# The first three weight units of a map, instead of two, run together over the arriving input tiles (second block of a two-block network on one NeuronCore)

## The chip, the cores and the metric

The kernel is one program on one core of a Trainium2 chip. The metric is device time in microseconds (us) of one execution; lower is better. TensorE (PE in the rows) does the matrix products, VectorE (DVE) and ScalarE (ACT) the elementwise work, GpSimd (POOL) almost nothing here, and SyncE (SP) issues nearly all DMAs.

## The reference, cut to what matters

The program computes two blocks one after the other over 512 positions of width 1024, all in float32. The second block, the one that is changed, is this, for two layers (`ab` in the first, `c` in the second):

```python
for layer in range(DEPTH):
    hn = rmsnorm(h, gains[0])
    mix = mixer_ab(hn, ...) if layer % 2 == 0 else mixer_c(hn, ...)   # each: hn @ w_in, attention-like work, @ w_out
    h = h + rmsnorm(mix, gains[1])
    hn = rmsnorm(h, gains[2])
    ff = jnp.square(jax.nn.relu(hn @ w_up[layer])) @ w_down[layer]    # 1024 -> 4096 -> 1024
    h = h + rmsnorm(ff, gains[3])
    gate = jax.nn.sigmoid(h @ w_ple_gate[layer])
    h = h + gate * (p[layer] @ w_ple[layer])
```

What matters is that each layer holds several large products `activations @ weights` (here called maps), most of them right behind a normalisation.

## The kernel before, in words

**A map.** Activations lie transposed: a tile is 128 features by 512 positions, and 1024 features are 8 tiles. Weights come as units of 128 x 1024 floats, each of which gives 128 output features from 8 input tiles. The function `linear` runs one map: `count` units over the tiles. Float32 precision is had from three products of rounded pieces: weights are split into a high part `WHI` (ScalarE, L378) and a rest `WLO` (VectorE, L387), activations in the same way, and each pair of unit and tile takes three matmuls of 128x512 (L431). So a unit is 8 x 3 = 24 matmuls.

**Weight buffers.** Units arrive by DMA in a ring of `SLOTS` = 2 buffers (`fetch`, L366), and are split into one of `WSLOTS` = 3 slots. `split_hi` waits until the unit that had the slot three units ago has been finished by TensorE (`units_done`); `fetch` waits until a ring buffer has been split (`w_lo`). Both engines run the same `turns`: before the first output, `split(c, eng, pos + WSLOTS)` makes the first three units ready as far as that has not been done; then for every finished unit `j` the output is taken off PSUM (`take`), unit `j + 3` is split, and the rest of the work on output `j` follows (`then`). A map ends by having split the first two units of the next map; the third is the one that the next map's own `turns` begins with.

**Order.** There is no scheduler. Each engine executes its instructions in the order in which the Python code emits them, block after block: `normalize` (or `pieces`) emits its ScalarE and VectorE work for all 8 tiles, and `linear`, called after it, emits `turns` behind that. On TensorE, `begin(j)` waits until the PSUM bank of unit `j` is free and its weights are split; `ready(k)` waits for the input tile `k`. The parameter `group` says how many units run together over the tiles as they arrive: tile 0 for each of them, then tile 1, and so on. The other units follow one by one:

```python
        for j in range(group):
            begin(j)
        for k in range(kt):
            pe.wait_ge(*ready(k))
            for j in range(group):
                products(j, k)
        for j in range(group, count):
            begin(j)
            for k in range(kt):
                products(j, k)
```

**What makes the tiles.** `normalize` (root of the mean square, then L694 scales a tile on VectorE, L683 rounds it on ScalarE, L707 takes the rest on VectorE) stands before `project_a`, `project_c` and the first up-projection of `ffn2`. `pieces` (L743 rounds on ScalarE, L750 takes the rest on VectorE) stands before `project_b` and `mix_out`. In `project_a` the outputs go through a convolution of four taps: L1647 on ScalarE, then three instructions of L1664 on VectorE, all of it in `take`, ahead of the next split. In `ffn2` the hidden width 4096 is worked off in four parts `p` of 8 units up and 8 down; only for the first part do the tiles still arrive, the other three find them ready.

Of the kernel before, what the change touches and what calls it, by code (L numbers as in the profile page):

```python
# [16 lines left out]
KT = D // P  # L17
NL, NC = 512, 256
# [119 lines left out]
def ffn_parts(hidden_tiles):  # L138

    return [(p, min(UB, hidden_tiles - p)) for p in range(0, hidden_tiles, UB)]  # L140
# [1493 lines left out]
def project_a(c, args, xp, ready):  # L1634

    CV = A2["CV"]
    tap3, taps, silu, zed = c.mark("act", 12), c.mark("dve", 36), c.mark("act", 12), c.mark("act", 4)
    cv = lambda j, lo, n: c.a(CV + (j % 4) * NL + lo, n)
    out = lambda j: c.a(A2["Q"] + j * NL, NL)
    tap = lambda k, j: c.vec(f"conv{k}", j)  # L1640

    def scalar(act, j, acc):
        a = acc[0][0]
        if j >= 12:
            act.activation(out(j), a, ACT.Silu).then_inc(*zed.up())
        else:
            act.activation(cv(j, 0, NL), a, ACT.Identity, scale=tap(3, j)).then_inc(*tap3.up())  # L1647

    def scalar2(act, j):
        if 1 <= j <= 12:  # L1650
            act.wait_ge(*taps.at(3 * j))
            act.activation(out(j - 1), cv(j - 1, 0, NL), ACT.Silu).then_inc(*silu.up())

    def vector(dve, j, acc):
        if j >= 12:
            return
        a = acc[0][0]
        dve.wait_ge(*tap3.at(j + 1))
        for z, k in enumerate((2, 1, 0)):
            d = 3 - k  # L1660
            if z:
                dve.wait_ge(*taps.at(3 * j + z))
            y = cv(j, d, NL - d)
            dve.scalar_tensor_tensor(y, a[:, 0:NL - d], tap(k, j), y, ALU.mult, ALU.add).then_inc(*taps.up())  # L1664

    linear(c, args, xp, KT, 16, NL, ready, lambda j: zed.at(j - 11) if j >= 12 else taps.at(3 * j + 3), scalar, vector, scalar2)


def project_b(c, args, xp, ready):

    done = c.mark("act", 16)

    def scalar(act, j, acc):
        i, m = j // 4, j % 4
        dst = c.a(A2[("Q", "K", "Z", "V")[i]] + m * NL, NL)
        if i == 2:
            act.activation(dst, acc[0][0], ACT.Sigmoid).then_inc(*done.up())
        else:
            act.activation(dst, acc[0][0], ACT.Copy, scale=SCALE2 if i == 0 else 1.0).then_inc(*done.up())
    linear(c, args, xp, KT, 16, NL, ready, lambda j: done.at(j + 1), scalar)  # L1680


def project_c(c, args, xp, ready):

    done = c.mark("act", 12)

    def scalar(act, j, acc):
        act.activation(c.a(place_c(j), NL), acc[0][0], ACT.Identity, bias=c.vec("b_qkv", j)).then_inc(*done.up())
    linear(c, args, xp, KT, 12, NL, ready, lambda j: done.at(j + 1), scalar)


def unit_norms(c, tiles_of, scales, eps=EPS, gain=None, times=None):
# [471 lines left out]
def place_c(j):  # L2164

    o = A3
    return o["Q"] + j * NL if j < 8 else o["K"] + (j - 8) * (NL + P) + P if j < 10 else o["VT"] + (j - 10) * NL
# [258 lines left out]
def mix_out(c, args, xp, ready, dst, bias=None):  # L2426

    squares = Squares(c, KT, NL, D)
    done = c.mark("act", KT)

    def scalar(act, j, acc):
        a = acc[0][0]
        if bias is None:
            act.activation(dst(j), a, ACT.Copy).then_inc(*done.up())
        else:
            act.activation(dst(j), a, ACT.Identity, bias=c.vec(bias, j)).then_inc(*done.up())

    def scalar2(act, j):
        squares.square(act, j, dst(j), done.at(j + 1))

    def vector2(dve, j):
        if j >= 2:
            squares.add(dve, j - 1)
    linear(c, args, xp, KT, KT, NL, ready, lambda j: done.at(j + 1), scalar, None, scalar2, vector2)
    return squares


# [41 lines left out]
def ffn2(c, args, l, late, last):  # L2489


    with c.pair(NL) as xp, c.pair(NL) as hidden, c.room(4 * NL) as room, c.room(2 * D) as wp, c.room(2 * NL) as pl, \
            c.room(KT * NL) as emb:
        hh, hl, hw = hidden
        y = lambda k: c.h(k)
        re = lambda j: room[:, (j % 4) * NL:(j % 4 + 1) * NL]
        ready = normalize(c, late, lambda k, q: c.vec(f"gain{l}2", k), xp)
        loaded = c.mark("dma", 2)
        block = c.stage()

        @block.sync
        def _(sp):
            sp.wait_ge(c.units_done, c.pos)
            sp.dma_start(wp[:], args["wple"][l]).then_inc(*loaded.up())
            sp.dma_start(pl[:], args["ple"][l]).then_inc(*loaded.up())
        full = lambda k: (c.units_done, c.pos)
        for p, m in ffn_parts(32):
            relu, made, hi, lo = c.mark("act", m), c.mark("dve", m), c.mark("act", m), c.mark("dve", m)
            done = c.mark("dve", KT)
            squares = Squares(c, KT, NL, D) if p + m == 32 else None  # L2510
            emptied = c.pos

            def scalar(act, j, acc):
                if j >= 4:
                    act.wait_ge(*lo.at(j - 3))
                act.activation(re(j), acc[0][0], ACT.Relu).then_inc(*relu.up())  # L2516

            def vector(dve, j, acc):
                dve.wait_ge(*relu.at(j + 1))
                dve.tensor_tensor(re(j), acc[0][0], re(j), ALU.mult).then_inc(*made.up())  # L2520

            def scalar2(act, j):
                act.wait_ge(*made.at(j + 1))
                if j == 0:
                    act.wait_ge(c.units_done, emptied)
                act.activation(hh[:, j * hw:j * hw + NL], re(j), ACT.Copy).then_inc(*hi.up())

            def vector2(dve, j):
                dve.wait_ge(*hi.at(j + 1))
                q = slice(j * hw, j * hw + NL)  # L2530
                dve.tensor_tensor(hl[:, q], re(j), hh[:, q].bitcast(F32), ALU.subtract).then_inc(*lo.up())
            linear(c, args, xp, KT, m, NL, ready, lambda j: made.at(j + 1), scalar, vector, scalar2, vector2)
            ready = full

            def take(dve, j, acc):
                a = acc[0][0]
                if p == 0:
                    dve.tensor_copy(y(j), a).then_inc(*done.up())
                else:
                    dve.tensor_tensor(y(j), y(j), a, ALU.add).then_inc(*done.up())  # L2540

            def square(act, j):
                if squares is not None:
                    squares.square(act, j, y(j), done.at(j + 1))

            def add(dve, j):
                if squares is not None and j >= 2:
                    squares.add(dve, j - 1)
            linear(c, args, hidden, m, KT, NL, lambda k: lo.at(k + 1), lambda j: done.at(j + 1), None, take, square, add)
        ready = add_normed(c, squares, f"gain{l}3", y, xp=xp)  # L2550
        return gated_embedding(c, args, l, xp, ready, loaded, wp, pl, emb, room, last)
# [60 lines left out]
def block2(c, args, late):  # L2612
# [28 lines left out]
    late = LateSquares(c, KT, NL, D)  # L2641
    add_normed(c, squares, "gain01", c.h, late=late)
    squares = ffn2(c, args, 0, late, False)
    o = A3
    with c.low_room(o["HIGH"]):
        with c.pair(NL) as xp:
            ready = normalize(c, squares, lambda k, q: c.vec("gain10", k), xp)
            project_c(c, args, xp, ready)
        with c.high_room(o["END"] - o["HIGH"]):
            positions(c, args)  # L2650
            finish_c(c)
            attention2(c)
    with c.pair(NL) as xp, c.room(KT * NL) as y:
        dst = lambda k: y[:, k * NL:(k + 1) * NL]
        squares = mix_out(c, args, xp, pieces(c, c.h, xp, NL), dst, "b_o")
        late = LateSquares(c, KT, NL, D)
        add_normed(c, squares, "gain11", dst, late=late)
    ffn2(c, args, 1, late, True)


# [124 lines left out]
```

## Time and profile before

| | us |
|---|---|
| median of 3 runs | 3949.96 |
| lowest, highest | 3944.89, 3950.35 |
| the profiled execution, as timed | 3958.45 |
| its span, first to last instruction | 3956.7 |
| TensorE busy in that span | 3468.1 |
| VectorE busy | 1715.6 |
| ScalarE busy | 1180.8 |

The profiled execution is one of its own and took 8.5 us more than the median. The profile gives for each instruction the start, the duration and, where the engine was idle before it, who ended the wait. A matmul's end is modelled and matmuls overlap, so that the distance between starts is what one costs; the granted clock is TensorE's, 1.00 for 2.4 GHz and 0.50 for 1.2 GHz. The second block takes the last 2,100 us of the span.

### The profile page before, as it was taken

The numbers are of one execution on the slowest core, as the hardware profiler recorded it, in microseconds if no ns is written. First come the engines' busy times: TensorE is split into PE (matmuls) and PEld (weight loads), VectorE is DVE, ScalarE is ACT, GpSimd is POOL, SyncE is SP. The second block draws the span as 40 slices with busy tenths as digits, with TensorE's granted clock in tenths as the row PEclk, the third lists the DMA queues.
The fourth block names the chain that finished last, engine by engine and source line by source line (L and its number), as shares of the span: only waits on it lengthen the run. The fifth ranks groups of instructions, "written<-read, shape, count | busy, mean of one in ns | idle before, by whom it ended". The sixth has DMA issues, their size and how long they took to land. (4 is left out here: it accounts for less than half of the span.)

```text
span 3956.7 us, 41490 instructions
## 1 busy us (share of the span) xinstructions
PE 3468.1 (88%) x16706; PEld 2741.9 (69%) x16706; DVE 1715.6 (43%) x2518; ACT 1180.8 (30%) x1919; POOL 98.5 (2%) x124
## 2 busy tenths in 40 slices
PE   7898999999989989998936769857999995889998
PEld 5555778888875568887725647646888674678886
DVE  2235454343544556445563232234444445544344
ACT  2134333131332444333321012103332332432222
POOL 0012100000001210000000000000000000000000
PEclk9899999999989999998967759557999997889999
DMA  6400033321221012322300002001232120022231
GB/s 245 167 1 1 30 110 119 141 103 59 68 76 53 1 43 91 101 96 75 99 0 3 2 0 85 1 0 59 91 102 96 59 90 20 16 81 91 96 99 61
DMA packets 74493, 270.21 MB, mean 68 GB/s; under 512 B 8256, under 2 KB 9920, under 8 KB 73024
## 3 DMA queue, kind: packets, MB, share of 16 engines
q1 hardware_dynamic: 74304, 267.57, 19.9%
q8 instruction: 134, 2.20, 0.2%
q14 instruction: 55, 0.45, 0.0%
HBM read 265.44 MB, written 2.10 MB: 68 GB/s over the span
## 5 line engine op out<-in xcount | busy, mean ns | idle before, releaser
L431 PE MATMUL PS<-room,WHI 128*128 128x512 f32 (+1 forms) x7184 | 2019.0, 378 | 88.4 <-DVE room L750 47.5
L431 PEld LDWEIGHTS PS<-room,WHI 128*128 128x128 f32 x7184 | 1273.0, 190 | 375.3 <-issue 126.8
L431 PE MATMUL PS<-room,WLO 128*128 128x512 f32 (+1 forms) x3592 | 1235.5, 374 | 0.0
L431 PEld LDWEIGHTS PS<-room,WLO 128*128 128x128 f32 x3592 | 636.4, 190 | 127.0
L387 DVE TENSOR_TENSOR WLO<-RING,WHI 128x1024 fp32r<-128x1024 f32 x370 | 452.2, 1222 | 427.9 <-ACT WHI L378 427.2
L378 ACT ACTIVATE WHI<-RING 128x1024 fp32r<-128x1024 f32 x370 | 389.0, 1054 | 549.0 <-PE PS L431 534.8
L831 DVE SCALAR_TENSOR_TENSOR H<-PS,VEC,H 128x511 f32<-128x511 f32 (+1 forms) x132 | 83.1, 657 | 307.9 <-ACT H L809 307.9
L809 ACT ACTIVATE H<-PS,VEC 128x512 f32<-128x512 f32 (+1 forms) x132 | 88.4, 703 | 349.4 <-PE PS L431 349.4
L1262 PE MATMUL PS<-room 96*128 96x256 f32 (+1 forms) x432 | 154.3, 476 | 11.2 <-ACT SQ L1373 7.7
L768 DVE SCALAR_TENSOR_TENSOR X<-PS,MOD,X 128x512 f32<-128x512 f32 x96 | 60.5, 658 | 221.3 <-PE PS L431 221.3
L1468 DVE TENSOR_REDUCE room<-PS 128x1 f32<-128x768 f32 (+1 forms) x120 | 101.9, 850 | 99.1 <-PE PS L1262 98.6
L2520 DVE TENSOR_TENSOR room<-PS,room 128x512 f32<-128x512 f32 x64 | 44.2, 691 | 180.3 <-ACT room L2516 120.0
L1262 PEld LDWEIGHTS PS<-room 96*128 96x128 f32 x432 | 73.8, 190 | 65.0 <-issue 51.2
L1285 PE MATMUL PS<-room 128*64 128x128 f32 x1248 | 82.5, 280 | 25.1 <-ACT room L1345 21.0
L2516 ACT ACTIVATE room<-PS 128x512 f32<-128x512 f32 x64 | 38.2, 596 | 212.7 <-PE PS L431 212.7
L1285 PEld LDWEIGHTS PS<-room 128*64 128x64 f32 x1248 | 68.2, 138 | 47.5 <-ACT room L1345 44.8
L1448 DVE COPY room<-PS 128x384 f32<-128x384 f32 (+1 forms) x120 | 59.5, 496 | 88.2 <-PE PS L1272 88.2
L2540 DVE TENSOR_TENSOR X<-X,PS 128x512 f32<-128x512 f32 x48 | 33.0, 687 | 135.3 <-PE PS L431 135.3
L617 PEld LDWEIGHTS PS<-ONES,SQ 128*128 128x128 f32 x288 | 62.3, 331 | 37.8 <-ACT SQ L606 10.0
L836 DVE SCALAR_TENSOR_TENSOR H<-PS,VEC,H 128x511 f32<-128x511 f32 (+1 forms) x132 | 83.2, 658 | 3.1
L617 PE MATMUL PS<-ONES,SQ 128*128 128x1 f32 x288 | 63.2, 353 | 23.6 <-DVE room L2459 9.1
L1188 PE MATMUL PS<-room 128*128 128x512 f32 (+1 forms) x210 | 77.8, 517 | 1.5 <-ACT SQ L1373 1.3
(318 smaller groups left out, 3258.4 us busy)
## 6 DMA issues: line engine op xcount, KB each, us to landing
RING<-in_stream SPq DMA_DIRECT2D x370, 512.0 KB, 3.3
room<-in_w_ada SPq DMA_DIRECT2D x84, 512.0 KB, 5.7
H<-in_w_ada SPq DMA_DIRECT2D x12, 512.0 KB, 4.6
room<-in_consts SPq DMA_DIRECT2D x4, 1024.0 KB, 9.7
room<-in_wq SPq DMA_DIRECT2D x2, 1728.0 KB, 7.7
X<-in_x_in SPq DMA_DIRECT2D x2, 1536.0 KB, 10.3
room<-in_consts SPq DMA_DIRECT2D x9, 256.0 KB, 4.7
room<-in_wple SPq DMA_DIRECT2D x2, 1024.0 KB, 4.8
```

Of the source, the lines that this page charges most:

```text
L378: act.activation(c.WHI[:, w:w + UN], c.RING[:, r:r + UN], ACT.Copy).then_inc(c.w_hi, 1)
L387: dve.tensor_tensor(c.WLO[:, w:w + UN], c.RING[:, r:r + UN], c.WHI[:, w:w + UN].bitcast(F32), ALU.subtract).then_inc(c.w_lo, 1)
L431: mm = pe.matmul(acc, wt[:, w], xt[:, k * xw + lo:k * xw + lo + q], start=(k == 0 and z == 0), stop=(k == kt - 1 and z == 2))
L617: mm = pe.matmul(c.bank(7, 1, NC + t), c.sq(k, self.n)[:, t * P:(t + 1) * P], c.ONES[:, 0:1], start=(k == 0 and t == 0), stop=(k == self.n ...
L768: ins = dve.scalar_tensor_tensor(x, a, mod(c, self.l, self.part, j, q), x, ALU.mult, ALU.add)
L809: ins = act.activation(cv(i, z, lo, w), a, ACT.Identity, bias=col("b_dw", j), scale=col("dw1_", j))
L831: ins = dve.scalar_tensor_tensor(y, a[:, 0:w - 1], col("dw0_", j), y, ALU.mult, ALU.add)
L836: ins = dve.scalar_tensor_tensor(y, a[:, 1:w], col("dw2_", j), y, ALU.mult, ALU.add)
L1188: mm = pe.matmul(c.bank(b + r, m), c.a(w + k * stride, P), c.a(x + k * W + lo, m), start=(k == 0), stop=(k == kn - 1))
L1262: mm = pe.matmul(c.bank(b + r, m), q_at(p, z, i * P, P, 0, 96), k_at(p, z, k0 + lo, m, 0, 96), start=True, stop=True)
L1285: mm = pe.matmul(c.bank(6 + part, P, (i % 4) * P, 64 * z, 64 * z + 64), c.a(vv + (t0 + t) * 768 + (2 * pair + z) * 64, 64), turned_at(a + ...
L1468: dve.tensor_reduce(c.a(NEG + j, 1), c.PS[:, 512 * b:512 * b + n], AX, ALU.max, negate=True).then_inc(*neg.up())
```

## The change

Seven calls of `linear` in the second block get `group=3` in place of the default of 2: those of `project_a`, `project_b`, `project_c`, of `mix_out` (used once in each layer), and of the first up-projection of `ffn2` (once in each layer). Down-projections, the other up-projections, the gated embedding and the first block keep two.

```diff
 def project_a(c, args, xp, ready):
...
-    linear(c, args, xp, KT, 16, NL, ready, lambda j: zed.at(j - 11) if j >= 12 else taps.at(3 * j + 3), scalar, vector, scalar2)
+    linear(c, args, xp, KT, 16, NL, ready, lambda j: zed.at(j - 11) if j >= 12 else taps.at(3 * j + 3), scalar, vector, scalar2, group=3)
...
 def project_b(c, args, xp, ready):
...
-    linear(c, args, xp, KT, 16, NL, ready, lambda j: done.at(j + 1), scalar)
+    linear(c, args, xp, KT, 16, NL, ready, lambda j: done.at(j + 1), scalar, group=3)
...
 def project_c(c, args, xp, ready):
...
-    linear(c, args, xp, KT, 12, NL, ready, lambda j: done.at(j + 1), scalar)
+    linear(c, args, xp, KT, 12, NL, ready, lambda j: done.at(j + 1), scalar, group=3)
...
 def mix_out(c, args, xp, ready, dst, bias=None):
...
-    linear(c, args, xp, KT, KT, NL, ready, lambda j: done.at(j + 1), scalar, None, scalar2, vector2)
+    linear(c, args, xp, KT, KT, NL, ready, lambda j: done.at(j + 1), scalar, None, scalar2, vector2, group=3)
...
 def ffn2(c, args, l, late, last):
...
-            linear(c, args, xp, KT, m, NL, ready, lambda j: made.at(j + 1), scalar, vector, scalar2, vector2)
+            linear(c, args, xp, KT, m, NL, ready, lambda j: made.at(j + 1), scalar, vector, scalar2, vector2, group=3 if p == 0 else 2)
```

No instruction is added or taken away, and VectorE, ScalarE, GpSimd and SyncE keep their orders. On TensorE the matmuls of the third unit move forward. The difference at the start of `project_a` (room23 and room24 are the high and low pieces of the input tiles, `dve_lane16` counts tiles made ready, `w_lo` the units split, `dve_lane12` stands for PSUM banks that came free):

```order
 L416 UNCONDITIONAL_BRANCH
-L431 MATMUL PS<-room23,WHI 128x512 [waits w_lo,dve_lane12,dve_lane16]
+L431 MATMUL PS<-room23,WHI 128x512 [waits dve_lane12,w_lo,dve_lane16]
 L431 MATMUL PS<-room24,WHI 128x512
 L431 MATMUL PS<-room23,WLO 128x512
```

The two lists of semaphores read alike, but the waits on `w_lo` that stand ahead of the first matmul are those of `begin(0)` and `begin(1)` before, and of `begin(0)`, `begin(1)` and `begin(2)` now. Where tile 7 ends, the wait that the third unit had for itself is gone:

```order
 L431 MATMUL PS<-room23,WHI 128x512 [waits dve_lane16]
-L431 MATMUL PS<-room24,WHI 128x512
-L431 MATMUL PS<-room23,WLO 128x512
-L431 MATMUL PS<-room23,WHI 128x512
-L431 MATMUL PS<-room24,WHI 128x512
-L431 MATMUL PS<-room23,WLO 128x512
-L431 MATMUL PS<-room23,WHI 128x512 [waits w_lo,dve_lane12]
```

Its matmuls now stand in threes behind those of the first two units, tile by tile, and the next wait on `w_lo` is the fourth unit's. On VectorE, at the same place, the order is this in both programs:

```order
L707 TENSOR_TENSOR room24<-X,room23 128x512 [waits act_lane23] x2
L468 UNCONDITIONAL_BRANCH
L387 TENSOR_TENSOR WLO<-RING,WHI 128x1024 [waits w_hi]
L1664 SCALAR_TENSOR_TENSOR room22<-PS,VEC,room22 128x511 [waits act_lane1,units_done]
L1664 SCALAR_TENSOR_TENSOR room22<-PS,VEC,room22 128x510 [waits dve_lane18]
L1664 SCALAR_TENSOR_TENSOR room22<-PS,VEC,room22 128x509 [waits dve_lane18]
L387 TENSOR_TENSOR WLO<-RING,WHI 128x1024 [waits w_hi]
```

The first L387 is the split of the third unit; it stands behind the last two tiles. The second is that of the fourth; it stands behind the three taps on the first unit's output. ScalarE has the same pattern:

```order
L683 ACTIVATE room23<-X 128x512 [waits dve_lane15] x8
L464 UNCONDITIONAL_BRANCH
L378 ACTIVATE WHI<-RING 128x1024 [waits units_done,ring_filled0]
L1647 ACTIVATE room22<-PS,VEC 128x512 [waits units_done]
L378 ACTIVATE WHI<-RING 128x1024 [waits units_done,ring_filled1]
```

All eight tiles come first, then the third unit's high part, then the first output and the fourth unit's high part.

## Rows read from the trace of the kernel before

**Rows 1.** The page, groups by line: xcount | busy us, mean ns | idle before, releaser.
```profile
L387 DVE TENSOR_TENSOR WLO<-RING,WHI 128x1024 fp32r<-128x1024 f32 x370 | 452.2, 1222 | 427.9 <-ACT WHI L378 427.2
L378 ACT ACTIVATE WHI<-RING 128x1024 fp32r<-128x1024 f32 x370 | 389.0, 1054 | 549.0 <-PE PS L431 534.8
```

**Rows 2.** Chain of waits, one part of the second feed-forward: start, us, what.
```profile
3610.44 88.16 PE PS L431 x384
```

**Rows 3.** Timeline of PE in project_a: start, us, instruction, count, [idle before <-releaser].
```profile
1875.41 1.19 PE L431 MATMUL PS<-room,WHI 128*128 128x512 f32 x2 [2.32 <-DVE room L707]
...
1888.12 0.62 PE L431 MATMUL PS<-room,WHI 128*128 128x512 f32 x2
```

**Rows 4.** The seven starts: us, matmuls busy (x), loads (x), granted clock, DMA, GB/s.
```profile
1875.41:1893.60 18.19, 18.19 (x72) 14.80 (x73) 0.90 0.13 38
...
sum 129.77, PE 129.77 PEld 105.52; mean PE 18.54 PEld 15.07
```

**Rows 5.** Timeline of DVE in project_a.
```profile
1882.14 1.47 DVE L707 TENSOR_TENSOR room<-X,room 128x512 fp32r<-128x512 f32 x2
1883.88 1.22 DVE L387 TENSOR_TENSOR WLO<-RING,WHI 128x1024 fp32r<-128x1024 f32 x1 [0.26 <-ACT WHI L378]
1888.43 2.32 DVE L1664 SCALAR_TENSOR_TENSOR room<-PS,VEC,room 128x511 f32<-128x511 f32 x3 [3.33 <-ACT room L1647]
1890.66 1.22 DVE L387 TENSOR_TENSOR WLO<-RING,WHI 128x1024 fp32r<-128x1024 f32 x1
```

**Rows 6.** L387 in windows, map's first matmul to third unit's split: us, DVE (x), clock.
```profile
1875.41:1885.10 9.69, 1.22 (x1) 0.82 0.00 0
2370.32:2375.51 5.19, 1.21 (x1) 0.66 0.01 3
2684.19:2689.39 5.20, 1.22 (x1) 0.64 0.00 0
2764.51:2774.19 9.68, 1.23 (x1) 0.73 0.01 2
3206.03:3215.72 9.69, 1.23 (x1) 0.79 0.00 0
3439.69:3444.89 5.20, 1.22 (x1) 0.50 0.00 0
3520.43:3530.11 9.68, 1.23 (x1) 0.81 0.00 0
sum 54.33, DVE 8.54; mean DVE 1.22
```

**Rows 7.** L387 in windows, end of six later matmuls to fourth unit's split.
```profile
1888.81:1891.88 3.07, 1.22 (x1) 1.00 0.00 0
2383.73:2385.43 1.70, 1.23 (x1) 1.00 0.00 0
...
sum 13.27, DVE 8.55; mean DVE 1.22
```

**Rows 8.** Timeline of the first gated embedding, where the third unit's split was late.
```profile
3159.55 1.23 DVE L387 TENSOR_TENSOR WLO<-RING,WHI 128x1024 fp32r<-128x1024 f32 x1 [18.92 <-ACT WHI L378]
...
3160.92 0.71 PE L431 MATMUL PS<-room,WHI 128*128 128x512 f32 x2 [2.98 <-DVE WLO L387]
```

**Rows 9.** Windows of PE: us, busy (x), granted clock, DMA, GB/s.
```profile
1875.41:1878.93 3.52, 3.52 (x8) 0.50 0.00 0
3439.69:3445.65 5.96, 5.96 (x14) 0.50 0.00 0
...
3162.35:3165.76 3.41, 3.41 (x9) 0.50 0.46 160
192.58:194.57 1.99, 0.01 (x2) 1.00 0.00 0
194.57:204.00 9.43, 9.43 (x26) 1.00 0.00 0
```

## The prediction, made before the changed kernel was run

> **What bounds the kernel now.** I looked first at the profile's groups by line for the price of making a unit ready: 1222 ns for the low part on VectorE and 1054 ns for the high part on ScalarE [rows 1]. Then the chain of waits: one part of a feed-forward is an unbroken run of TensorE, 384 matmuls in 88.16 us, so 0.2296 us each and 5.51 us a unit [rows 2]. In the maps of the second block the time is TensorE's, and a delay of TensorE there is a delay of the end, because the stage after a map waits for its last unit.
>
> The change wants to give TensorE more work for each arriving tile. So the next question is whether TensorE is short of work while tiles arrive. I laid a window over the first 72 matmuls (three units) of each of the seven maps [rows 4]. TensorE is busy from end to end in all of them: together 129.77 us for 504 matmuls. At 0.2296 us these are 115.7 us; the other 14.1 us are the low clock at a map's start, since a map begins at 0.50 and goes to 1.00 after 3.5 to 6.0 us (the shortest and the longest [rows 9]; the others lie at 3.55, 3.71, 3.73, 4.11 and 5.31; the sum of the seven is 29.9 us, of which half, 15.0, is lost). The low clock accounts for all of the excess. There is no hunger for tiles that a third unit could still: with six matmuls on a tile it is already never out of work once it has begun. **The gain open to the change is nil.**
>
> **What the change adds at a map's start.** TensorE executes in order, and `begin(2)` now stands ahead of tile 0: it waits until the third unit is split. That split is not made early. Its instructions are emitted behind the eight tiles on both engines. In `project_a` TensorE begins at 1875.41 [rows 3], when tile 0 is there; VectorE ends the last two tiles from 1882.14 on, waits 0.26 us for ScalarE's high part, and only then makes the low part, 1883.88 to 1885.10 [rows 5]. None of that moves, since neither engine waits for TensorE in this stretch. So the new start is 1885.10 and not 1875.41. Windows from each map's first matmul to the end of that split give the seven distances: 9.7 us for the four behind `normalize`, 5.2 us for the three behind `pieces`, in sum 54.33 us [rows 6]. From the end of a split to TensorE's start it takes another 0.14 us (a split that ends at 3160.78 and a matmul at 3160.92 [rows 8]), seven times 1.0. Behind the wait TensorE has the same 72 matmuls to do. **First term: 54.33 + 1.0 = 55.3 us.**
>
> That such a wait is real is shown by the gated embedding, where the third unit's split stands behind ScalarE's earlier work too: TensorE sat idle for 2.98 us until WLO was there [rows 8]. All that is new is that the wait comes before the first tile and not behind the last.
>
> **What it adds behind the group.** The fourth unit needs the first one's slot. With two together, the first unit ends, and the third one's 24 matmuls (5.5 us) hide the taking of the output and the split of the fourth. With three together, only six matmuls, 1.4 us, are left when the first unit ends. In `project_a` the third unit's first matmul starts at 1888.12 [rows 3]; the first unit's last one is four places earlier, and six more after that carry TensorE to 1888.12 + 3 x 0.23 = 1888.81. The fourth unit's split ends at 1891.88, since the three taps, 2.32 us, stand ahead of it on VectorE [rows 5]: a distance of 3.07. In the other six the take is one short instruction beside the high part, and the distance is 1.61 to 1.80 us; in sum 13.27 us [rows 7], and seven times 0.14 on top. **Second term: 14.3 us.** It ends there: the fifth unit's split needs, even in `project_a`, only three more taps and itself (2.32 + 1.22 = 3.5 us [rows 5]), and TensorE takes 5.5 us for the fourth. The bound on the other side is zero, if these splits came earlier against TensorE than now; nothing moves them, so I take the full sum.
>
> **What it does to the clock.** (a) The seven low-clock starts come again, at another moment each. They took 3.5 to 6.0 us, and a later start draws anew in that range: all at the short end would give 2.6 us back (29.9 less 7 x 3.53, halved), all at the long end cost 5.9 more. I take the middle, 4.75 us each, which is +1.7. (b) A stall can drop the clock: the 2.98 us of [rows 8] were followed, from 3162.35 on, by 3.41 us at 0.50 [rows 9], which is 1.7 us lost. The stall of 3.2 us in `project_a` is nearest to that, so 1.7 is taken. The other six are 1.8 to 1.9 us; the nearest row is a stall of 1.98 us amid dense matmuls after which 9.4 us ran at 1.00 [rows 9], so nothing is taken, and 10.2 is kept as the upper bound. **Third term: 1.7 + 1.7 = 3.4 us.**
>
> Here the Trainium skill speaks for the change. Its page "Perfetto Trace Analysis", section "Matmul Optimizations", says that matmuls should run back to back in batches because the engine's power follows its utilization; nine at a time on a tile would be the better batch. By that rule the rises would come sooner, and the sum would be 4.3 us less than with my 1.7. The trace bears it out in so far as a stretch after idleness is slow, but in the windows of [rows 4] the six-at-a-time form is already without gaps, so the batch is not made denser. The Trainium skill's page "TensorE: Matmul & The Clock Gate", section "What's actually happening", adds that the slow start is an amount of time and not a number of matmuls; here 8 matmuls and 14 matmuls preceded the rise [rows 9], which agrees.
>
> **The sum** is 55.3 + 14.3 + 3.4 = 73.0 us. The profiled execution took 3958.45 and would take 4031.5; it ran 8.5 above the median of 3949.96, so for the median I say 3950 + 73 = **4023**. Nothing is costed at zero but the other engines' work, which keeps its order and is waited for by nobody earlier than now.
>
> **Rivals.**
> 1. *The forecast*, 4023: front waits, stalls, one clock drop.
> 2. *All stalls drop the clock.* For it: a stall of 2.98 us did. Against: one of 1.98 us did not. It gives 4023 + 10.2 = 4033.
> 3. *The front wait isn't there*, because the third unit's split is done in time. Then only the stalls and the clock stay: 3950 + 14.3 + 3.4 = 3968. For it: a map ends with two units split, and a third slot comes free with its last unit. Against: the order of both engines, and the end at 1885.10 [rows 5].
> 4. *Not slower, through the clock.* Place: the first matmuls of the seven maps. If nine matmuls a tile raised the clock at once after 3.5 us everywhere, 2.6 us would come back, and the time would be 3947 if nothing else were lost. It decides from the point at which front waits and stalls together cost less than those 2.6 us, against 69.6 by the windows. This is the Trainium skill's rule on batches ("Perfetto Trace Analysis") carried to its end.
> That the change doesn't do what it says is ruled out by the order: the third unit's matmuls stand among the others in all seven maps.
>
> **How the numbers follow.** Chances: forecast 0.86, second 0.08, third 0.03, fourth 0.02, anything else 0.01. Low end: 3950 + 69.6, less 2.6 for short rises, less 5 as the runs reach down to 3944.89: 4012. High end: 3950 + 69.6 + 5.9 + 1.7 + 10.2 = 4037. About 0.2% (8 us) is what a measurement of this kernel can tell from no change. Only the fourth case falls within it, and none is faster by more: faster 0.01, same 0.02, slower 0.97.
>
> **What would show it.** In each of the seven maps the first matmul is released by WLO and not by a tile, 0.14 us after a split that ends behind the last tile; TensorE's idle time ahead of it is 9.8 us longer behind `normalize` and 5.3 us behind `pieces`. After 72 matmuls there is a gap of 3.2 us in `project_a` and of 1.8 to 1.9 us in the six others, again ended by WLO. The distance from the first matmul to the end of the 72 stays at 18 to 20 us. Everything else keeps its lengths. The forecast is wrong if TensorE starts a map before the eighth tile is done, if a stage after a map has slack that swallows the delay, or if the gaps behind the group go on from unit to unit.

## The result, and the profile after

| | before | after |
|---|---|---|
| median, us | 3949.91 (3944.89 to 3950.35, 4 runs) | 4020.36 (4016.19 to 4029.48, 4 runs) |
| ratio, 95% interval | | 1.0184 (1.0165 to 1.0204) |
| span of the profiled execution | 3956.7 | 4019.6 |
| TensorE busy | 3468.1 | 3463.4 |

The change costs 70 us; 4023 had been forecast. TensorE does the same work in the same busy time, so what was added is idle time. In the profile's groups by line it stands at the matmul of the maps. The same line before and then after (after the bar: busy us, mean ns | idle before, and what ended most of it):

```profile
L431 PE MATMUL PS<-room,WHI 128*128 128x512 f32 (+1 forms) x7184 | 2019.0, 378 | 88.4 <-DVE room L750 47.5
```

```profile
L431 PE MATMUL PS<-room,WHI 128*128 128x512 f32 (+1 forms) x7184 | 2020.6, 378 | 157.7 <-DVE WLO L387 132.0
```

The idle time has grown by 69.3 us. Of the 157.7 us, 132.0 are now ended by VectorE's split of a weight unit, L387. The waits of TensorE in the second block, before and then after (waiting <- releaser: us, times, longest):

```profile
PE PS L431 <- DVE room L750: 47.5, 3, 22.2
PE PS L431 <- DVE room L707: 9.3, 4, 2.3
PE PS L431 <- DVE WLO L387: 6.0, 2, 3.0
```

```profile
PE PS L431 <- DVE WLO L387: 132.0, 16, 27.7
```

Before, seven maps began when a tile came (L750, L707), and the split was waited for twice, in the gated embeddings. After, no map with three units begins on a tile: the split ends 16 waits, which are seven starts, seven stalls behind the group and the same two embeddings.

The start of `project_a` after, first VectorE, then TensorE (answers to [rows 5] and [rows 3]):

```profile
1880.79 1.47 DVE L707 TENSOR_TENSOR room<-X,room 128x512 fp32r<-128x512 f32 x2
1882.51 1.23 DVE L387 TENSOR_TENSOR WLO<-RING,WHI 128x1024 fp32r<-128x1024 f32 x1 [0.25 <-ACT WHI L378]
...
1902.20 2.32 DVE L1664 SCALAR_TENSOR_TENSOR room<-PS,VEC,room 128x511 f32<-128x511 f32 x3 [18.47 <-ACT room L1647]
1904.44 1.22 DVE L387 TENSOR_TENSOR WLO<-RING,WHI 128x1024 fp32r<-128x1024 f32 x1
```

```profile
1883.99 1.20 PE L431 MATMUL PS<-room,WHI 128*128 128x512 f32 x2 [12.25 <-DVE WLO L387]
...
1905.80 1.19 PE L431 MATMUL PS<-room,WHI 128*128 128x512 f32 x2 [3.05 <-DVE WLO L387]
```

The idle time ahead of the map has gone from 2.32 to 12.25 us. The split begins behind the last two tiles, as before; only now TensorE waits for it. After 72 matmuls comes the second gap, 3.05 us, until the fourth unit is split behind the three taps. The same window as in [rows 4], from the first matmul to the 73rd, for the first and the last of the seven maps and in sum:

```profile
1883.99:1905.79 21.80, 18.76 (x72) 14.96 (x73) 0.89 0.07 24
...
3580.51:3601.06 20.55, 18.97 (x72) 15.01 (x73) 0.90 0.07 26
sum 146.81, PE 133.74 PEld 106.17; mean PE 19.11 PEld 15.17
```

Before it was 129.77 us with no idle time; now it is 146.81.

### The profile page after: what moved, and what is told of

Same layout as the page of the kernel before. It is cut to its first block and busy times, and to the rows that moved or that the text cites. A ratio compares the mean times of both kernels' runs of the same rounds, so it can differ in the third digit from the quotient of the medians.

```text
span 4019.6 us, 41490 instructions
## 1 busy us (share of the span) xinstructions
PE 3463.4 (86%) x16706; PEld 2738.8 (68%) x16706; DVE 1715.0 (43%) x2518; ACT 1180.6 (29%) x1919; POOL 98.5 (2%) x124
## 5 line engine op out<-in xcount | busy, mean ns | idle before, releaser
L431 PE MATMUL PS<-room,WHI 128*128 128x512 f32 (+1 forms) x7184 | 2020.6, 378 | 157.7 <-DVE WLO L387 132.0
L387 DVE TENSOR_TENSOR WLO<-RING,WHI 128x1024 fp32r<-128x1024 f32 x370 | 452.1, 1222 | 466.8 <-ACT WHI L378 466.1
```

The source lines that it names most:

```text
L387: dve.tensor_tensor(c.WLO[:, w:w + UN], c.RING[:, r:r + UN], c.WHI[:, w:w + UN].bitcast(F32), ALU.subtract).then_inc(c.w_lo, 1)
L431: mm = pe.matmul(acc, wt[:, w], xt[:, k * xw + lo:k * xw + lo + q], start=(k == 0 and z == 0), stop=(k == kt - 1 and z == 2))
```

## The experiments

Eight kernels ran after the result, the first four on one chip and the last four on another, each set beside runs of the kernel before.

**The changed kernel again.**

> The changed kernel once more, to part what the change costs from what varies by itself. By the first pair of traces the seven front waits (56.2 us), the seven stalls behind the group (14.3 us) and the clock at the maps (about 4 us) add up to 74 us, while the medians are 70.4 us apart and the two profiled spans 62.9. Theory (the rest is the clock of the delta, mLSTM and attention phases, which is drawn anew in each execution): fourteen gaps of the same length within 0.1 us each, a ratio of 1.016 to 1.020, and other lengths of the phases between the maps than in the first trace. Rival (the later start is given back somewhere): the same phases are short again, by the same amounts as in the first trace, some 11 us in all.

Measured: 4015.22 (4013.22 to 4022.95, 4 runs) against 3950.24 (3942.22 to 3960.39, 11 runs), ratio 1.0166 (1.0147 to 1.0185). The seven front waits were again 12.25 behind `normalize` and 27.69, 27.86 and 8.48 behind `pieces`, the stalls again 3.05, 1.69, 1.69, 1.61, 1.77, 1.78 and 1.59 us. All agree with the first trace within 0.16 us (0.1 had been expected). The question was why the two first spans lay only 62.9 us apart when the parts at the maps sum to some 74. Nearly all of the 12 us lies in three places. The first is the stretch from `project_a`'s last matmul to the last norm ahead of `project_b` (gates, delta rule); it was 4.2 us shorter after. In order: before; after; after again; and `g3_pieces`, a kernel told of below whose program is the kernel before's up to the end of this stretch (columns: length, PE busy (x), granted clock, DMA, GB/s):

```profile
1965.21:2348.08 382.87, 236.08 (x1024) 0.65 0.02 5
```
```profile
1978.89:2357.53 378.64, 231.84 (x1024) 0.66 0.02 5
```
```profile
1975.93:2349.38 373.45, 225.95 (x1024) 0.68 0.02 5
```
```profile
1963.60:2329.55 365.95, 220.49 (x1025) 0.69 0.02 6
```

The same 1,024 matmuls took 366 to 383 us, and the shorter the time, the higher the mean clock. The extremes are of two kernels that are identical up to there, so this is not the change's doing; the kernel before happened to be profiled with the longest of the four. The second place is the like stretch in the second layer, between `project_c` and `mix_out`, with 4.3 us; before and then after:

```profile
3274.10:3436.67 162.57, 107.03 (x541) 0.78 0.02 6
```
```profile
3321.98:3480.29 158.31, 104.70 (x540) 0.78 0.02 7
```

The expected form of the theory, other lengths in the second trace, holds for these two; that each was short in the first changed trace for this reason and no other isn't shown.

The third place is not chance alone, and in it the rival (something is given back) is right. From the 73rd matmul of `project_b` to the front wait of `mix_out`, and from the 73rd matmul there to the front wait of `project_c`, before and then after:

```profile
2388.53:2661.96 273.43, 220.40 (x793) 0.65 0.08 27
2702.48:2762.18 59.70, 48.33 (x217) 0.75 0.23 79
```
```profile
2405.92:2677.81 271.89, 218.81 (x792) 0.65 0.09 29
2726.68:2785.19 58.51, 47.14 (x216) 0.77 0.28 90
```

Together they are 2.7 us shorter after, and 4.8 us shorter in the again-run (269.48 and 58.86). The ten traces on record fall into two groups. In the four in which these two maps run one or two units together, the lengths are 273.3 to 273.4 and 59.7 us. In the six in which they run three, they are 268.6 to 271.9 and 58.2 to 59.1 us, at a mean clock that is higher by up to 0.03. It does not go with how late a map starts: `g3_early` below, whose maps start at most 1.6 us late, has the shortest of all (268.61 and 58.15). Why the clock stands higher there is not shown.

**Only behind normalize, only behind pieces.** The first kernel leaves `project_b` and `mix_out` as before, the second changes them alone. The first one's edit, against the changed kernel:

```diff
 def project_b(c, args, xp, ready):
...
-    linear(c, args, xp, KT, 16, NL, ready, lambda j: done.at(j + 1), scalar, group=3)
+    linear(c, args, xp, KT, 16, NL, ready, lambda j: done.at(j + 1), scalar)
 def mix_out(c, args, xp, ready, dst, bias=None):
...
-    linear(c, args, xp, KT, KT, NL, ready, lambda j: done.at(j + 1), scalar, None, scalar2, vector2, group=3)
+    linear(c, args, xp, KT, KT, NL, ready, lambda j: done.at(j + 1), scalar, None, scalar2, vector2)
```

> Three units together only in the four maps behind normalize (project_a, project_c, the first up-projection of each ffn2); project_b and mix_out keep two. Theory (a front wait as long as eight tiles take, and a stall behind the group): fronts 4 x 9.9 = 39.8, stalls 3.2 + 1.8 + 1.9 + 1.8 = 8.7, one clock drop 1.5, together 50 us: 3950 + 50 = 4000. Rival (each of the seven maps pays about the same, since the price is that of a start at the low clock): 4/7 of 70 = 40 us: 3990.

Measured: 4001.3 (3996.23 to 4003.09), ratio 1.0127 (1.0108 to 1.0145), so 50 us more than before (43 to 57).

> The other half: three units together only in project_b and in both mix_out, behind pieces. Theory: fronts 3 x 5.5 = 16.4, stalls 1.8 + 1.8 + 1.9 = 5.6, together 22 us: 3972. Rival (the same price for each map): 3/7 of 70 = 30 us: 3980.

Measured: 3974.42 (3959.66 to 3978.92), ratio 1.0052 (1.0033 to 1.0071), so 20.5 us (13 to 28). The waits of TensorE in that trace show both kinds of start side by side:

```profile
PE PS L431 <- DVE WLO L387: 75.0, 8, 27.7
PE PS L431 <- DVE room L707: 9.3, 4, 2.3
```

The four untouched starts still end on a tile (L707, 9.3 us as before), the three others on the split. 50 and 20.5 make 70.5, the whole. The rival, one price for each map, wanted 40 and 30; it misses both intervals. The cost of a map goes with the time that its tiles take.

**The third unit's split ahead of the tiles** (`early` is set in the four calls of `normalize` in the second block):

```diff
 def normalize(...):
     def _(act):
+        if early:
+            split_hi(c, act, c.pos + WSLOTS)
         for k in range(nk):
...
     def _(dve):
+        if early:
+            split_lo(c, dve, c.pos + WSLOTS)
         dve.wait_ge(*spread.at(1))
 def pieces(c, source, xp, n, nk=KT):
     def _(act):
+        split_hi(c, act, c.pos + WSLOTS)
...
     def _(dve):
+        split_lo(c, dve, c.pos + WSLOTS)
```

> Three units together in all seven maps, as in the changed kernel, but the third unit is split ahead of the tiles: in normalize while VectorE and ScalarE wait for the root to be spread, in pieces ahead of tile 0. Theory: behind normalize the front wait is gone and nothing takes its place (0 instead of 39.8), behind pieces 1.0 to 1.6 us a map remain, because the split (1.05 and 1.22 us) now delays tile 0 (4 instead of 16.4); the stalls behind the group stay (14.3) and so does a clock drop (1.5): 3950 + 20 = 3970. Rival A (the front wait is only a symptom, the price is in running three): 4020. Rival B (three together over the tiles do gain once the wait is gone): below 3964, what the stalls alone give.

Measured: 3967.47 (3961.87 to 3977.73), ratio 1.0044 (1.0027 to 1.0062), so 17.5 us (11 to 24) instead of 70. In the timeline of VectorE the split now lies in the time in which it waits for TensorE to spread the root:

```profile
1869.90 1.23 DVE L387 TENSOR_TENSOR WLO<-RING,WHI 128x1024 fp32r<-128x1024 f32 x1 [0.77 <-ACT WHI L378]
1871.37 1.41 DVE L696 SCALAR_TENSOR_TENSOR X<-H,VEC,PS 128x512 f32<-128x512 f32 x2 [0.24 <-PE PS L644]
```

```profile
1873.65 0.77 PE L431 MATMUL PS<-room,WHI 128*128 128x512 f32 x1 [2.32 <-DVE room L711]
```

TensorE starts 2.32 us after its last norm matmul, on a tile (L711 is L707 moved by the added lines), exactly as in [rows 3]. Behind `pieces` the idle times are 23.85, 23.85 and 4.64 us against 22.2, 22.2 and 3.02 before: 1.6 us a map, the upper end of what was expected. The front wait was thus the split's place in two queues. The result lies within noise of rival B's bound of 3964, which this run alone does not rule out; the one after next does.

**Each unit finished by itself over the last four tiles.**

```diff
-        for k in range(kt):
+        both = kt if group < 3 else kt // 2
+        for k in range(both):
             pe.wait_ge(*ready(k))
             for j in range(group):
                 products(j, k)
...
+        for j in range(group):
+            for k in range(both, kt):
+                if j == 0:
+                    pe.wait_ge(*ready(k))
+                products(j, k)
```

> Three units together in the seven maps over the first four tiles only; over the last four each unit is finished by itself, so that the first unit ends 24 matmuls (5.5 us) ahead of the third and not 6 (1.4 us). The front wait stays. Theory: the stalls behind the group (14.3 us) and the clock drop after the longest of them (1.5) go, since 5.5 us are more than the 3.0 to 4.6 us from the first unit's end to the fourth unit's split; the fronts (56.2) and the later clock rises (2.4) stay: 3950 + 58 = 4008. Rival (the stall comes from the third slot as such and stays): 4020.

Measured: 4006.29 (4002.69 to 4008.44), ratio 1.0151 (1.0138 to 1.0164), so 60 us (54 to 65). By the ratios that is 13 and 6 us less than the two results of the changed kernel, against 12 expected. The interval of the second overlaps with this one, so the times alone do not decide it; the trace does. The window of `project_a`, first matmul to the 73rd:

```profile
1886.39:1904.60 18.21, 18.21 (x72) 14.83 (x73) 0.90 0.09 29
```

It has no gap, with the same number of slots. Nor have the other six; of the 16 waits on L387 nine are left, the seven starts and the two embeddings. So the stall came from the first unit's late end and not from three slots being too few as such. (Four slots were not tried.)

**Both repairs at once.**

> Both repairs at once: the third unit split ahead of the tiles, and each unit finished by itself over the last four tiles. What is left of the change is the idea itself, more work for each arriving tile. Theory (TensorE is never short of tiles with two units, so the idea has nothing to gain): only the delay of tile 0 behind pieces remains, 3 x 1.4 = 4 us: 3954. Rival (the denser work pays once its price is gone): 3945 or below, and the excess over 0.2296 us a matmul in the first 72 of a map falls below the 14.1 us of the kernel before.

Measured: 3953.03 (3942.38 to 3960.16, 11 runs) against 3948.13 (29 runs), ratio 1.0009 (0.9996 to 1.0023). The windows over the first 72 matmuls of the seven maps sum to

```profile
sum 131.44, PE 131.43 PEld 106.57; mean PE 18.78 PEld 15.22
```

against 129.77 in [rows 4]. There is no idle time in them, as there was none before, and the excess over 0.2296 us a matmul is 15.7 us and not below 14.1. Not every cost is gone: behind `pieces` TensorE waits 52.5 us where it waited 47.5. The 5.0 us agree with the 3.6 measured (-1.6 to 9), so three units over the tiles give nothing that these runs can tell from zero. Rival B falls, and so does the idea that denser batches raise the clock sooner: it rose 3.6 to 5.8 us after the seven starts, against 3.5 to 6.0 before.

**One unit over the tiles** (`group=1` in the calls that the change set to 3, in the kernel before).

> The other direction: one unit over the arriving tiles in the seven maps, the others behind it. Three matmuls a tile are 0.69 us at full clock, less than the 1.26 us that VectorE takes for a tile behind normalize (0.61 behind pieces). Theory: behind normalize TensorE is short of tiles now and the map loses what it waits: the first unit ends with tile 7 at 9.2 us after the start, the second and third 11.0 us later at 20.2 if the clock is high, against 18.2 to 19.0 before, so 1 to 2 us in each of four maps and up to 1.7 more where the gaps delay the rise of the clock; behind pieces nothing: 3950 + 4 to 14, middle 3958. Rival (the group size does not matter in either direction, all is the third split): 3950.

Measured: 3956.34 (3945.26 to 3964.01, 12 runs), ratio 1.0021 (1.0008 to 1.0035), so 8 us more than before (3 to 14). In `project_a` TensorE now does run short of tiles:

```profile
1879.74 0.73 PE L431 MATMUL PS<-room,WHI 128*128 128x512 f32 x2 [0.29 <-DVE room L707]
...
1881.00 0.74 PE L431 MATMUL PS<-room,WHI 128*128 128x512 f32 x2 [0.29 <-DVE room L707]
```

Its starts are 1.26 us apart, VectorE's pace for a tile; these gaps exist with three matmuls a tile and are absent with six, so behind `normalize` two is where the hunger ends. Behind `pieces`, with a tile every 0.61 us, one unit is already enough: the 72 matmuls of `project_b` took 18.15 us and those of the first `mix_out` 18.27, against 18.20 and 18.28 before. The map `project_a` took 91.6 us in place of 89.8. In the profiled pair the seven maps sum to only 3 us more than before (one `mix_out` began at the high clock and saved 2.8), so the size of 8 us rests on the timed runs.

**The third unit's split earlier in the gated embedding,** with two units as before:

```diff
             for m in range(KT):
+                if m == 2:
+                    split_hi(c, eng, c.pos + WSLOTS)
                 eng.wait_ge(*summed.at(m + 1))
```

> Two units together as before; one thing else: in both gated embeddings ScalarE makes the third unit's high part between its second and third copy, where it waits 2.5 us for TensorE anyway, and not behind all eight. Theory (a split that stands behind other work is what TensorE waits for): the two stalls of 2.98 us go, and with them up to 1.7 us each of low clock behind them: 3950 less 6 to 9.4, so 3941 to 3944. Rival (the split now delays the copies, whose two PSUM banks the woven products need, or the fourth unit is late instead): 3950 or more.

Measured: 3939.68 (3925.42 to 3952.0, 12 runs) against 3948.13, ratio 0.9983 (0.9969 to 0.9996), so 7 us less (2 to 12). Three rows of its trace answer to [rows 8]; the first two are ScalarE's and VectorE's, the third the window from the map's first matmul to the fall of the clock behind it:

```profile
3129.30 1.06 ACT L378 ACTIVATE WHI<-RING 128x1024 fp32r<-128x1024 f32 x1
```
```profile
3130.39 1.23 DVE L387 TENSOR_TENSOR WLO<-RING,WHI 128x1024 fp32r<-128x1024 f32 x1 [1.23 <-ACT WHI L378]
```
```profile
3118.00:3181.70 63.70, 61.11 (x224) 0.96 0.20 66
```

The split is done at 3131.6, some 14 us before the third unit's first matmul (3145.91), and the wait of TensorE on L387 has gone from the list in both embeddings. No low clock follows in the window; its mean of 0.96 comes from the 5.6 us at 0.50 with which the map begins. This version beats both kernels.

## Why the prediction was right, point by point

- **No gain to be had.** Right: with the costs removed but for 5.0 us of idle time, the ratio is 1.0009 (0.9996 to 1.0023), and the windows of the first 72 matmuls are no shorter.
- **First term, the front waits, 55.3 us.** The seven idle times grew from 56.8 to 112.9 us, by 56.2. TensorE starts 0.25 to 0.28 us after the split's end (1883.73 to 1883.99 in `project_a`) and not 0.14, which had been read where it was waiting in the middle of a map; that is the 0.9. The experiments bear out the cause (17.5 us of cost where the split is early) and how it goes with the tiles (50 and 20.5).
- **Second term, the stalls, 14.3 us.** The windows grew by 17.0 us (129.77 to 146.81), of which 2.4 are the later rise of the clock. That leaves 14.6. The idle times themselves are 3.05 us and 1.59 to 1.78, in sum 13.2, and not the 3.2 and 1.8 to 1.9 forecast, because the last matmul before a gap is shown with 0.39 us where the sum had reckoned 0.23. The gap did not go on from unit to unit.
- **Third term, the clock, 3.4 us.** The rises took 3.8 to 6.2 us after the starts, in sum 34.7 in place of 29.9: 2.4 us lost where 1.7 was taken. The again-run's sum was 30.7: 0.4 lost. Two executions of one kernel thus differ by 2 us here, so how much of this term comes true is luck, and 6.2 lies outside the range of 3.5 to 6.0 that the forecast had read. The prediction also took 8 and 14 matmuls before the rise as a sign that an amount of time decides; the same two rows take 3.52 and 5.96 us, so that neither is fixed. The drop behind the 3.05 us stall came:

```profile
1905.43:1908.83 3.40, 3.03 (x7) 0.50 0.44 151
```

  It is what the forecast had, 3.4 us at 0.50. It began before TensorE went on, so that 3.03 us of work fell in it and 1.5 us were lost where 1.7 was taken; in the again-run, with 6.11 us of work, it was 3.1. The six shorter stalls were followed by no drop, in this trace or in the again-run. The second rival (all of them drop, 4033) is out.
- **The third rival,** no front wait, 3968, is nearly what `g3_early` made real, at 3967 (with 4.9 us of waits left behind `pieces`). **The fourth,** a gain through the clock, is refuted by `g3_early_half`.
- **The sum.** 56.2 + 14.6 + 2.4 + 1.5 makes 74.7 us at the maps, and 74.3 in the again-run. The medians differ by 70.4 us in the first comparison and by 65.0 in the second, whose intervals are 65 to 81 and 58 to 73; the second does not hold 75. What the forecast had at nothing is the last step, "everything else keeps its lengths": the two stretches behind `project_b` and `mix_out` gave back 2.7 and 4.8 us. That makes 72.0 and 69.5, which lie in both intervals. So 73.0 came as near as it did because this term and the terms that were a little too small offset each other in part, which was luck. The range, 4012 to 4037, holds both medians and all eight runs. The step of adding a term to the profiled execution's own time worked less well than the terms did: 3958.45 + 73 = 4031.5, and the profiled run took 4021.4, because phases that the change does not touch vary by up to 17 us.

## What to carry to other kernels

Before more work is put on arriving inputs, look whether the engine idles between them, and whether all that the larger batch needs is ready at its start: a batch waits for its last member, so one preparation that is emitted behind the inputs turns an overlap into a sequence. Then look at what the batch's first member was hiding when it ended early. Where an engine waits for a preparation that another engine could have made in its own idle time, move the preparation: two such moves gave about 50 of the 70 us, and 7 us, here.

## What the runs showed of the hardware that was not expected

The drop of the clock after a stall is not fixed by the stall's length. The gap of 2.98 us in the first gated embedding cost 3.4 us at 0.50 in the trace before [rows 9], and in the trace after, with the same length, nothing (columns: length, PE busy (x), granted clock, DMA, GB/s):

```profile
3193.68:3196.67 2.99, 0.01 (x2) 1.00 0.00 0
3196.67:3229.00 32.33, 32.33 (x141) 1.00 0.36 117
```

The 3.05 us stall of `project_a` was followed by 3.4 us of low clock in the trace after and by at least 6.7 in that of the again-run:

```profile
1900.80:1907.50 6.70, 6.11 (x15) 0.50 0.51 159
```

Over all the traces on record, the stall of 2.98 us in the first embedding had a drop within 1.5 us of its end in five of nine, the same stall in the second in eight of nine, and the 3.05 us stall of `project_a` in four of four. Of the 24 stalls of 1.59 to 1.78 us behind a group none had one.

And the delta-rule phase, with the same instructions, ran at a mean clock of 0.65 to 0.69 and took 366 to 383 us. That is a spread of 17 us, where the 29 timed runs of the kernel before in the last comparison span 25 us.
